# Samples' values, residual products and gate weighting moved in a hybrid decoder layer with dense PEER experts

## The reference

```python
z = x @ w_in                                  # q, k, v of both mixers, gates
o_a = stick_breaking(q_a, ..., k_a, v_a)      # 8 heads x 64; samples over 256 cached rows + 4 new
o_b = nsa_attend(...)                         # compressed, selected and window branches
m = concat(rms(o_a) * g_a, rms(o_b) * g_b) @ w_out
h = layer_norm(ALPHA * x + m)
# PEER: 8 heads, 16 of 128*128 experts for each token
q = (h @ w_q).reshape(C, 8, 2, 128)
s1, i1 = top_k(q[:, :, 0] @ keys0.T, 16);  s2, i2 = top_k(q[:, :, 1] @ keys1.T, 16)
top_s, e = top_k(s1[..., None] + s2[..., None, :], 16)
g = softmax(top_s);  a = gelu(einsum('cpkd,cd->cpk', u_tab[e], h))
f = einsum('cpk,cpkd->cd', g * a, v_tab[e])
y = layer_norm(ALPHA * h + f)
```

## Time and profile before

| | us |
|---|---|
| median of 3 runs (lowest, highest) | 1116.89 (1115.89, 1117.94) |
| profiled execution | 1112.11 |
| its span | 1110.4 |
| PE busy | 1065.4 (96%) |
| DVE busy | 865.0 (78%) |
| ACT busy | 551.2 (50%) |
| POOL busy | 260.1 (23%) |
| down stage, first product to end of span | 732.70 to 1110.4 |

### The profile page before, as it was taken

How to read it: one execution, slowest core, us unless ns; L and a number is a source line. 1 busy time by engine, 2 the same in 40 slices (tenths; PEclk the granted TensorE clock), 3 DMA queues, 4 the chain that set the end, 5 groups by cost and what they waited for, 6 DMA issues and landing times.

```text
span 1110.4 us, 23617 instructions
## 1 busy us (share of the span) xinstructions
PE 1065.4 (96%) x7264; PEld 953.6 (86%) x7264; DVE 865.0 (78%) x1808; ACT 551.2 (50%) x1054; POOL 260.1 (23%) x281
## 2 busy tenths in 40 slices
PE   6999989979999999999999999989999999999996
PEld 6997646969999999999999999978777787888875
DVE  4325364668988988888459999969888998987877
ACT  5325556344544444434555555545455555555543
POOL 0244302000001000554000000025455554533320
PEclk9999998989999999999999999999999999999998
DMA  7656921423468766999863444459889998977762
GB/s 259 268 192 194 346 92 48 170 77 116 153 209 280 251 232 232 346 413 397 312 218 119 142 142 142 142 186 307 306 288 302 306 300 294 302 243 246 243 215 90
DMA packets 96249, 253.19 MB, mean 228 GB/s; under 512 B 11424, under 2 KB 44224, under 8 KB 95408
## 3 DMA queue, kind: packets, MB, share of 16 engines
q1 hardware_dynamic: 81840, 196.84, 52.1%
q0 software_dynamic: 14368, 55.87, 13.9%
HBM read 232.60 MB, written 22.12 MB: 229 GB/s over the span
## 4 chain that ended last, share of the span: by engine, by line
PE 79%; DVE 7%; DMA 6%; issue 4%; POOL 2%; ACT 2%; DVEq 0%; SPq 0%; ACTq 0%; POOLq 0%
PE ps L557 14%; PE ps L558 14%; PE ps L559 14%; PE ps L990 7%; PE ps L992 7%; PE ps L991 7%; PE ps L971 5%; DMA activations<-u_out 4%; DVE w_lo L1360 3%; PE ps L641 1%; DVE sacc L1804 1%; POOL vrow L518 1%; PE ps L917 1%; POOL a_in L522 1%; DMA a_in<-activations 1%
## 5 line engine op out<-in xcount | busy, mean ns | idle before, releaser
L1360 DVE TENSOR_TENSOR w_lo<-ring,w_hi 128x512 fp32r<-128x512 f32 (+1 forms) x458 | 433.5, 956 | 111.6 <-ACT w_hi L1044 96.5
L1044 ACT CAST w_hi<-ring 128x512 fp32r<-128x512 f32 (+1 forms) x460 | 343.4, 751 | 97.5 <-PE ps L992 51.7
L557 PE MATMUL ps<-h_hi,w_hi 128*128 128x256 f32 (+1 forms) x1152 | 339.3, 295 | 6.0 <-DVE h_lo L1631 4.9
L558 PE MATMUL ps<-h_lo,w_hi 128*128 128x256 f32 (+1 forms) x1152 | 328.7, 285 | 0.0
L559 PE MATMUL ps<-h_hi,w_lo 128*128 128x256 f32 (+1 forms) x1152 | 326.8, 284 | 0.0
L557 PEld LDWEIGHTS ps<-h_hi,w_hi 128*128 128x128 f32 x1152 | 219.6, 191 | 10.7 <-DVE h_lo L1631 5.3
L558 PEld LDWEIGHTS ps<-h_lo,w_hi 128*128 128x128 f32 x1152 | 219.1, 190 | 0.0
L559 PEld LDWEIGHTS ps<-h_hi,w_lo 128*128 128x128 f32 x1152 | 217.3, 189 | 0.0
L990 PE MATMUL ps<-w_hi,y_hi 128*128 128x512 f32 x512 | 201.4, 393 | 11.3 <-DVE y_lo L1792 10.4
L992 PE MATMUL ps<-w_lo,y_hi 128*128 128x512 f32 x512 | 199.8, 390 | 0.0
L991 PE MATMUL ps<-w_hi,y_lo 128*128 128x512 f32 x512 | 199.7, 390 | 0.0
(11 more groups left out here) (337 smaller groups left out, 1216.4 us busy)
## 6 DMA issues: line engine op xcount, KB each, us to landing
ring<-in_uT_dram SPq DMA_DIRECT2D x128, 512.0 KB
ring<-in_v_dram SPq DMA_DIRECT2D x128, 512.0 KB
activations<-u_out SPq DMA_DIRECT2D x128, 128.0 KB
a_in<-activations SPq DMA_DIRECT2D x128, 128.0 KB
ring<-in_w_in_dram SPq DMA_DIRECT2D x22, 512.0 KB
ring<-in_w_q_dram SPq DMA_DIRECT2D x16, 512.0 KB
ks<-in_cache_sb_dram POOLq DMA_DIRECT2D x16, 256.0 KB, 3.2
vs<-in_cache_sb_dram POOLq DMA_DIRECT2D x16, 256.0 KB, 5.5
```

Of the source, the lines that this page charges most:

```text
L557: mm(out, hi, hi_, start=start, stop=False)
L558: mm(out, hi, lo_, start=False, stop=False)
L1044: nc.scalar.copy(w_hi[slot][:, x], ring[:, ring_slot, x]).then_inc(part_hi, 2 if half is None else 1)
L1360: V.tensor_tensor(w_lo[slot][:, x], ring[:, ring_slot, x], w_hi[slot][:, x].bitcast(F32), ALU.subtract).then_inc(part_lo[ring_slot], 2 if ...
```

## The change

Three edits and a new layout for some tiles.

1. `ss_values` is cut in parts. The first group's third part goes from behind round 1 to behind round 2; of the second group one part stands behind round 3 and two behind round 4; `ss_tokens` goes from round 5 to round 6. VectorE's `ss_picked(0)` goes from round 2 to round 3, ahead of `np_out(0)`.
2. The residual products no longer use hsum. TensorE multiplies h_hi and h_lo apart with the scaled identity, 32 products, bank by bank as the gelus free them, ahead of the wait for the gates and of expert 0. The scaled identity is made before the one-hot loop, in a place of its own; `with_lows` and hsum are gone.
3. `weigh` goes from GpSimd to VectorE: in the round of expert j, between the first w_lo half and y_lo of j, VectorE weighs expert j+1. GpSimd keeps only the gathers. Rows are added behind four of every 16 experts, so that rows 2 to 29 go with experts 7, 11, ... 115, and rows 30 and 31 behind experts 116 and 117.

```diff
@@ GpSimd
-            for j in range(4):
-                weigh(j, slice(j, j + 1), 16)
-                if j >= 2:
-                    row_in(j, j, j - 1)
-            for i in range(5):
-                for r in range(16):
-                    n = 4 + 16 * i + r
-                    weigh(r % 4, slice(n, n + 1), 16 * (n // 4 + 1))
-                    if r in ROW_IN:
...
+            for m in range(2, SLOTS):
+                row_in(m, m, m - 1)
@@ TensorE, attention
                 if u == 1:
                     pe.wait_ge(ss_w, 1)
-                    ss_values(0)
+                    ss_values(0, 0)
+                    pe.wait_ge(v_in[0], 16 * 8)
+                    ss_values(0, 1)
+                if u == 2:
+                    ss_values(0, 2)
                 if u == 3:
-                    ss_values(1)
-                if u == 5:
+                    pe.wait_ge(ss_pick, 1)
+                    ss_values(1, 0)
+                if u == 4:
+                    pe.wait_ge(v_in[1], 16 * 8)
+                    ss_values(1, 1)
+                    ss_values(1, 2)
+                if u == 6:
                     ss_tokens()
@@ TensorE, down stage
+            pe.wait_ge(id_scaled, 1)
+            for bank in range(4):
+                tok = slice(bank // 2 * 128, bank // 2 * 128 + 128)
+                pe.wait_ge(u_act, 4 + NE - 3 + bank)
+                for part in (h_hi, h_lo):
+                    for c in range(4):
+                        ins = mm(ps[:, bank, c * 128:(c + 1) * 128], part[:, bank % 2 * 4 + c, tok].bitcast(F32),
+                                 scaled_id[:, :], start=part is h_hi and c == 0, stop=False, skip_group_check=True)
+            ins.then_inc(f_mm, 1)
             pe.wait_ge(g_sb, 4 + DT // 4)
-            pe.wait_ge(u_act, 4 + NE)
...
-            pe.wait_ge(h_sum, 2)
-            for tt in range(2):
-                for c in range(KD):
-                    ins = mm(ps[:, 2 * tt + c // 4, c % 4 * 128:(c % 4 + 1) * 128], hsum[:, c, tt * 128:(tt + 1) * 128],
-                             scaled_id[:, :], start=False, stop=False, skip_group_check=True)
-            ins.then_inc(f_mm, 1)
@@ VectorE
-                if u == 2:
+                if u == 3:
                     ss_picked(0)
...
+            def weigh(r, j, arrived):
+                dve.wait_ge(a_full[r], arrived)
+                V.tensor_tensor(a_in[:, r, :].unsqueeze(1), a_in[:, r, :].unsqueeze(1), gates[:, j, :],
+                                ALU.mult).then_inc(y_mul, 1)
+
-            def lows_down(i, j):
+            def lows_down(i, j, weigh_next=True):
 
                 low_half(i, AT_V + j, 0)
+                if weigh_next:
+                    weigh((j + 1) % 4, bass.ds(4 * i + j + 1, 1), 16 * i + 16 * ((j + 1) // 4 + 1))
                 low_y(j, 4 * i + j + 1)
                 low_half(i, AT_V + j, 1)
...
-            with dve.Fori(0, 5) as i:
+            with dve.Fori(0, 7) as i:
                 for r in range(16):
                     lows_down(4 * i, 4 + r)
-                    if r in ROW_ADD:
...
+                    if r % 4 == 3:
+                        m = r // 4
+                        add_row(m % 2, sgate[:, bass.ds(4 * i + (2 + m), 1)], 32 * i + 16 * (m // 2 + 2), 4 * i + (2 + m))
+            for r in range(4):
+                lows_down(0, NE - 12 + r)
+                if r < 2:
+                    m = SLOTS - 2 + r
+                    add_row(r, sgate[:, m:m + 1], 16 * (m // 2 + 1), m)
```

More of the change, by code:

```diff
@@ L296, in trunk @@
         assert at_x + 8 * T <= at_h
-        hsum = at("hsum", [128, KD, T], at_h)
-        scaled_id = at("scaled_id", [128, 128], rest)
+        scaled_id = at("scaled_id", [128, 128], at_x + 8 * T - 128)
         stats = at("stats", [128, 3, 2, 6], rest + 128)
@@ L790, in np_values, with ss_values @@
                 ins.then_inc(np_pv, 1)
-            def ss_values(w):
-                if w == 1:
-                    pe.wait_ge(ss_pick, 1)
-                pe.wait_ge(v_in[w], 16 * 8)
-                for p in range(3):
-                    for b in range(4):
-                        rows = slice(32 * b, 32 * b + 32)
-                        c = w * 128 + 32 * b
-                        if p == 0:
-                            ins = mm(ps[rows, 7, 0:512], zss[0:32, 512 + c:544 + c], vnat[0:32, 2, 0:4, :],
-                                     start=True, stop=False)
-                        else:
-                            ins = mm(ps[rows, 7, 0:512], zss[:, (p - 1) * 256 + c:(p - 1) * 256 + c + 32],
-                                     vs[w][:, 2 * b + p - 1, :], start=False, stop=p == 2)
-                ins.then_inc(ss_pv, 1)
+            def ss_values(w, part):
+                for b in range(4):
+                    rows = slice(32 * b, 32 * b + 32)
+                    c = w * 128 + 32 * b
+                    if part == 0:
+                        ins = mm(ps[rows, 7, 0:512], zss[0:32, 512 + c:544 + c], vnat[0:32, 2, 0:4, :],
+                                 start=True, stop=False)
+                    else:
+                        ins = mm(ps[rows, 7, 0:512], zss[:, (part - 1) * 256 + c:(part - 1) * 256 + c + 32],
+                                 vs[w][:, 2 * b + part - 1, :], start=False, stop=part == 2)
+                if part == 2:
+                    ins.then_inc(ss_pv, 1)
             def ss_tokens():
@@ L989, in part @@
                     out = ps[:, 2 * tt + half, :]
-                    mm(out, hi, w_hi[slot][:, x], start=start, stop=False)
-                    mm(out, lo, w_hi[slot][:, x], start=False, stop=False)
-                    return mm(out, hi, w_lo[slot][:, x], start=False, stop=stop)
+                    mm(out, hi, w_hi[slot][:, x], start=start, stop=False, skip_group_check=True)
+                    mm(out, lo, w_hi[slot][:, x], start=False, stop=False, skip_group_check=True)
+                    return mm(out, hi, w_lo[slot][:, x], start=False, stop=stop, skip_group_check=True)
                 if stop:
@@ L1005, in _ @@
             for r in range(4):
[L1006 to L1012 removed]
+                experts_down(r, halves(0, AT_V + r), r + 1, False, False)
             with pe.Fori(1, NE // 4 - 2) as i:
@@ L1770, in _ @@
             dve.wait_ge(s_act, 1)
+            V.tensor_scalar(scaled_id[:, :], k("ident"), ALPHA, None, ALU.mult).then_inc(id_scaled, 1)
             link(V.tensor_tensor(sgate[:, :], sgate[:, :], sact[:, :], ALU.mult))
@@ L1804, in add_row @@
                 V.scalar_tensor_tensor(sacc[:, :], vrow[:, q, :], gate, sacc[:, :], ALU.mult, ALU.add).then_inc(v_acc, 1)
-            def with_lows(c):
-                V.tensor_tensor(hsum[:, c:c + 4, 0:DT], h_hi[:, c:c + 4, 0:DT].bitcast(F32),
-                                h_lo[:, c:c + 4, 0:DT].bitcast(F32), ALU.add).then_inc(h_sum, 1)
             dve.wait_ge(g_sb, 4 + DT // 4)
+            for j in range(2):
+                weigh(j, slice(j, j + 1), 16)
             low_half(0, AT_V + 1, 1)
             low_y(0, 1)
+            weigh(2, slice(2, 3), 16)
             low_y(1, 2)
-            V.tensor_scalar(scaled_id[:, :], k("ident"), ALPHA, None, ALU.mult)
             dve.wait_ge(vg_in[0], 16)
```

32 lines of the change are left out of this document (6 added, 26 removed).

## The result

Faster: the fast comparison gives 0.9927 of the time before, 95% interval 0.9904 to 0.9951. The changed kernel's median is 1112.7 us (20 runs, 1105.97 to 1119.65) beside 1118.0 for the kernel before (20 runs taken with them, 1114.2 to 1128.0). On the 1116.89 us of the runs shown the ratio makes 1108.7 us (1106.2 to 1111.4): a gain of 8.2 us where 10.8 were forecast, so the forecast of 1106.1 lies just outside the low edge.

A forecast was written before the change was run, and what follows sets the result against it. TensorE, busy 96% of the span, was taken as the bound, waiting in the down stage on a late VectorE. The terms -2.2 - 9.2 + 0.6 = -10.8 us took 1116.89 to 1106.1 us, with 8 in 10 from 1102 to 1112.5.

The forecast's parts named there:

- The residual products, -2.2: Start of the down stage: residual products fill TensorE's wait and avoid the slow clock; expert 4 2.2 us sooner.
- The weighing, -9.2: Experts 4 to 119: weighing on VectorE ends TensorE's waits; of 10.2 us lost, 1.0 comes back.
- the second rival: Down stage: VectorE becomes the bound if a weighing costs over 0.88 us; 1119.3 us at 1.00; chance 0.05.
- The third: Down stage: the load of a_in, now in VectorE's path, holds the loop; 1163 us, or 1125; chance 0.03.
- The last rows, +1.0: Near expert 118: VectorE waits for the last gathered rows, costing TensorE 1.0 us (0 to 2).
- The samples' values, +0.6: Attention stage: splitting and reordering the samples' values delays the samples' transposes by 0.6 us (-1.5 to +1.5).
- rival 4: Attention and down stages: the split fills TensorE's gaps and the last rows don't hold VectorE; 1103.0 us; chance 0.12.
- The sum, -10.8: Whole kernel: residual products, weighing and samples' values together, -2.2 - 9.2 + 0.6 us.

The follow-up runs named there:

- e3_residual_only: The kernel before with only the residual products moved ahead of the gates' wait, weighing still on GpSimd: ratio 1.0025 (0.9985 to 1.0064) to the kernel before.
- e9_gpsimd_reads: The kernel after plus an unused 128x256 product on GpSimd for each of experts 4 to 115: ratio 1.0106 to the kernel before, 1.8% slower than the kernel after.
- e10_row15_later: The kernel before with the sixth of each six row gathers issued one weighing later on GpSimd: ratio 1.0005 to before, experts 4 to 119 in 322.48 us.
- e8_two_more_on_vector: The kernel after plus two unused 128x256 products on VectorE per expert, 4 to 115: ratio 1.0275 to before, experts 4 to 119 in 361.3 us.

## Why the prediction was right, by its steps

- **The residual products, -2.2:** measured -2.17, with the products where they were forecast and no fall of the clock. Expert 4 came at 759.56 and not near 746, since all ahead of it was late, but 18.17 us behind the last one-hot group where 18.1 was forecast. Shown by the traces alone, and 1.4 of it is the clock that no longer falls; the rest needs the weighings on VectorE too (e3_residual_only). The comparison of times for e3_residual_only shows no gain.
- **The weighing, -9.2:** measured -8.74. The size was right. Of the reason, the larger part is shown (e9_gpsimd_reads brings the long instructions back, and the waits with them), and a part was missing: 3.2 us came from weighings queued behind a gather that waited for VectorE (e10_row15_later). The move removes both at once, which is why the sum still held; the prediction knew only the first, so in this part it was luck. VectorE's need per expert was right to 0.01 us (e8_two_more_on_vector), so the second rival was far off. The third, the load that holds the loop, shows as three waits of VectorE, 3.4 us in all, one of them 2.45. The prediction took its 7.56 us for a load of the stretch with six rows in sixteen; it was the one behind SP's load of 1024 KB.
- **The last rows, +1.0:** charged near 118; the trace of after lost nothing there, its sisters 0.26 (no split), 0.75 (no split, copy ahead) and 1.03 (weighing alone). The 1.3 that were lost are the late load at expert 15, so that this term came out by luck.
- **The samples' values, +0.6:** +0.75 in the trace up to the scores of u=5. At equal clock the split alone is 1.5 us slower than the kernel before, and the kernel after 1.3 slower than the one without it; neither is apart from 0.6 within its bounds. That is against the half of rival 4 by which the split fills gaps (-1.5); its other half, that the last rows don't hold VectorE, held in the trace of after.
- **The sum, -10.8:** the interval's middle is -8.2, and the traces' parts make -2.17 - 8.74 + 0.75 = -10.2. Some 2 us are missing. The clock can hold most of it: without the fall near 732 us the mean clock should be higher by 0.0015 (0.5 x 3.4 in 1113, an estimate), worth 1.4 to 1.7 us, but the runs of both kernels have 0.984 to 0.985. At equal clock the parts make -0.75 - 8.74 + 0.75 = -8.7, beside 8.1 ± 1.3 measured. Why the mean clock didn't rise is open; the bounds on the difference of the two means are as wide as the missing 0.0015. The split's extra microsecond may be one; the up stage may be another, where the 14 profiles, of equal code there, took 346.5 to 352.5 us from the first product of h to the one-hot products. The three first profiles with the weighing on VectorE all took over 351.6, against 348.4 to 350.3 without; a later one with it took 346.5, so that the weighing isn't the reason. The length goes with the time at which the stage begins (230 to 245 us, correlation 0.87 over the 14): profiles with more half clock ahead of it are also longer in it. It isn't settled further.

## What to carry to other kernels

Price work on an engine by the starts of its instructions while it is behind, and check what is queued behind each instruction that waits: a gather that waits for another engine's sum holds every weighing behind it. A product with two SBUF inputs on GpSimd beside two-input VectorE instructions costs both (here GpSimd's took 945 ns and not 740, VectorE's w_lo 1139 and not 684); where VectorE has the room, moving it there can make VectorE's total smaller. And where single profiles differ by microseconds in a stretch that the edit doesn't touch, look at the granted clock of that stretch before any story.

## What the hardware showed that was not expected

Moving 128 weighings onto VectorE made VectorE less busy (865.0 us before, 851.7 after), since w_lo and y_lo shrank by more than the weighings add (behind the one-hot products -46.9 and -13.2 us, +53.6; the two additions into hsum, 2.4, are gone too, and the records of neighbours overlap).

A gather's issue on GpSimd depends on how full VectorE is. In the kernel after it takes 1.15 us in the median. With GpSimd's extra product, VectorE nearly without a pause, it is 3.06; with two more products on VectorE 10.5, and once 22.1. Tile vrow of that last kernel, and the timeline of one such gather:

```profile
L517 POOL DMA_INDIRECT vrow<-in_v_dram,expert x30: 944/10476/22122, 747.5 to 1104.6; - x30
```

```profile
869.76 22.12 POOL L517 DMA_INDIRECT vrow<-in_v_dram,expert  x1 [0.65 <-DVE sacc L1805]
...
897.73 1.28 DVE L1805 SCALAR_TENSOR_TENSOR sacc<-vrow,sgate,sacc 128x1024 f32<-128x1024 f32 x1 [6.66 <-DMA vrow<-in_v_dram,expert]
```

From 869.76 to 891.06 VectorE never paused. Then it stood still, for this very row, and 0.82 us later, at 891.9, the gather ended; the row came late, VectorE waited 6.66 us and TensorE with it. All four gathers of 22.12 us in this trace end 0.82 us behind the start of such a pause: each engine stood there for the other. The Trainium skill ("SBUF — State Buffer", Who interferes with whom) says that `tensor_tensor` was not seen to stall a DMA that GpSimd issues. This trace disagrees, at least for an indirect one: VectorE ran nothing but two-input instructions there. Which of the gather's steps is held wasn't tried.
